# Attention over the memory with operands in rounded high and low parts

## What is computed

```
q = (h @ w_mq)      in 4 heads of 256
k = (mem_n @ w_mk), v = (mem_n @ w_mv)
p = softmax(q k^T * 256 ** -0.5)
y = (p v) @ w_mo
```

## Time and profile before

| | us |
|---|---|
| median of 3 runs | 900.39 |
| lowest, highest | 900.27, 903.83 |
| the profiled execution | 900.8 |
| its span, first to last instruction | 899.0 |
| PE busy in it | 883.5 (98%) |
| DVE busy, ACT busy | 574.6, 511.4 |

### The profile page before, as it was taken

The page is one execution under the profiler, slowest core; times in us unless marked ns, Lnnn a source line. Parts: engine busy times, 40 slices in busy tenths (PEclk is TensorE's granted clock), DMA queues, the critical chain, the costliest instruction groups (busy, mean ns, idle before and its releaser), DMA issues.

```text
span 899.0 us, 14674 instructions
## 1 busy us (share of the span) xinstructions
PE 883.5 (98%) x5696; PEld 783.3 (87%) x5696; DVE 574.6 (64%) x903; ACT 511.4 (57%) x937; POOL 90.2 (10%) x111
## 2 busy tenths in 40 slices
PE   8999999999999999999999999999999999999998
PEld 7898977898899998887778889988899789998886
DVE  6456666654676664445656999989846576664443
ACT  6466666665666553336558668797255466554330
POOL 0010000010000000001000413360152101000000
PEclk9999999999999999999999999999999999999999
DMA  9865324464456665555354644354430366655562
GB/s 331 301 198 203 141 96 141 140 212 94 151 178 193 195 222 199 198 188 187 130 199 149 197 145 149 115 185 141 114 134 1 120 206 186 193 188 187 189 198 80
DMA packets 110395, 152.22 MB, mean 169 GB/s; under 512 B 6752, under 2 KB 68344, under 8 KB 109944
## 3 DMA queue, kind: packets, MB, share of 16 engines
q1 hardware_dynamic: 110328, 151.31, 51.6%
HBM read 147.99 MB, written 3.30 MB: 168 GB/s over the span
## 4 chain that ended last, share of the span: by engine, by line
issue 47%; PE 33%; DVE 9%; ACT 3%; DMA 3%; POOL 2%; POOLq 1%; DVEq 1%; ACTq 0%; SPq 0%
PE acc L465 4%; PE acc L467 4%; PE acc L466 4%; PE acc L478 4%; PE acc L477 4%; PE acc L479 4%; DVE s_w_lo L415 3%; ACT s_w_hi L409 1%; DVE s_qkvT L1554 1%; PE acc L524 1%; PE acc L526 1%; PE acc L525 1%; DMA s_w_raw<-in_w_out 1%; POOLq L664 1%; ACT s_relu_i L1477 1%
## 5 line engine op out<-in xcount | busy, mean ns | idle before, releaser
L415 DVE TENSOR_TENSOR s_w_lo<-s_w_raw,s_w_hi 128x2048 fp32r<-128x2048 f32 (+1 forms) x201 | 313.1, 1574 | 170.1 <-ACT s_w_hi L409 169.8
L409 ACT ACTIVATE s_w_hi<-s_w_raw 128x2048 fp32r<-128x2048 f32 (+1 forms) x201 | 263.3, 1331 | 144.4 <-PE acc L467 100.7
L477 PE MATMUL acc<-s_h_hi,s_w_hi 128*128 128x256 f32 x784 | 218.6, 279 | 0.0
L478 PE MATMUL acc<-s_h_lo,s_w_hi 128*128 128x256 f32 x784 | 216.9, 277 | 0.0
L479 PE MATMUL acc<-s_h_hi,s_w_lo 128*128 128x256 f32 x784 | 216.9, 277 | 0.0
L477 PEld LDWEIGHTS acc<-s_h_hi,s_w_hi 128*128 128x128 f32 x784 | 147.4, 188 | 0.4
L478 PEld LDWEIGHTS acc<-s_h_lo,s_w_hi 128*128 128x128 f32 x784 | 147.3, 188 | 0.3
L479 PEld LDWEIGHTS acc<-s_h_hi,s_w_lo 128*128 128x128 f32 x784 | 147.2, 188 | 0.0
L466 PE MATMUL acc<-s_w_lo,s_hid_hi 128*128 128x512 f32 x224 | 87.1, 389 | 0.0
L467 PE MATMUL acc<-s_w_hi,s_hid_lo 128*128 128x512 f32 x224 | 87.1, 389 | 0.0
L465 PE MATMUL acc<-s_w_hi,s_hid_hi 128*128 128x512 f32 x224 | 87.1, 389 | 0.0
(11 more groups left out here) (334 smaller groups left out, 1459.1 us busy)
## 6 DMA issues: line engine op xcount, KB each, us to landing
s_w_raw<-in_w_in SPq DMA_DIRECT2D x43, 1024.0 KB, 5.2
s_w_raw<-in_w_ff SPq DMA_DIRECT2D x32, 1024.0 KB, 5.2
s_w_raw<-in_w_mlp_up SPq DMA_DIRECT2D x16, 1024.0 KB, 5.4
s_w_raw<-in_w_mlp_down SPq DMA_DIRECT2D x16, 1024.0 KB, 5.0
s_w_raw<-in_w_out SPq DMA_DIRECT2D x8, 1024.0 KB, 5.7
s_w_raw<-in_w_mk SPq DMA_DIRECT2D x4, 1024.0 KB, 5.7
s_w_raw<-in_w_mv SPq DMA_DIRECT2D x4, 1024.0 KB, 5.3
s_w_raw<-in_w_mq SPq DMA_DIRECT2D x4, 1024.0 KB, 5.2
```

Source lines behind the costliest of these rows:

```text
L409: act.activation(w_hi[u % SPLIT_SLOTS][:, cs], w_raw[u % RAW_SLOTS][:, cs], ACT.Copy).then_inc(w_hi_done, 4 if q is None else 1)
L415: dve.tensor_tensor(w_lo[u % RAW_SLOTS][:, cs], w_raw[u % RAW_SLOTS][:, cs], w_hi[u % SPLIT_SLOTS][:, cs].bitcast(F32), ALU.subtract).then ...
L477: pe.matmul(o, wh[:, cs], hi[:, k, :], start=k == 0, stop=False)
L478: pe.matmul(o, wh[:, cs], lo[:, k, :], start=False, stop=False)
```

## The change

Queries, keys, probabilities and values become high and low parts of type fp32r, and each product of the attention over the memory becomes three. The new buffers lie over others that are free by then (`mkT_hi` and `mkT_lo` over the normed memory `m_hi` and `m_lo`, `mv_hi` over keys and values of the first attention, `mv_lo` over its bias table).

- Keys: ACT rounds `mkT` in two instructions of 128x1024 ahead of `ff_act`, and DVE takes the remainder in two ahead of `ff_dve`.
- Values: ACT rounds `mv` in two of 128x1024 behind `ff_act`, ahead of the rounding of `mq[2]`. DVE's two remainders stand behind the one of `mq[2]`.
- Queries: ACT's copies out of PSUM now write `mqT_hi`. DVE gets four instructions for `mqT_lo`.
- Probabilities: DVE's copy (L850) becomes a copy on ACT (`PT_hi`) and a subtraction on DVE (`PT_lo`) behind it.
- PE: the first transposes of probabilities (pair 0) stand ahead of the scores of pair 1. Scores and values are 12 single-pass products for a pair in place of 4 of f32.

```diff
+        def mq_act_hi(act, j):
+            u = of["mq"][j]
+            act.wait_ge(unit_done, u + 1)
+            act.activation(mqT_hi[:, 2 * j:2 * j + 2, :], acc[units[u]["banks"][0]][:].rearrange("p (c s) -> p c s", c=2), ACT.Copy,
+                           scale=0.0625).then_inc(mq_hi, 1)
...
+        def mem_act_hi(act, keys, g):
+
+            if keys:
+                act.activation(mkT_hi[:, 4 * g:4 * g + 4, :], mkT[:, 4 * g:4 * g + 4, :], ACT.Copy).then_inc(mem_hi, 1)
+            else:
+                act.activation(mv_hi[:, g, :], mv[:, g, :], ACT.Copy).then_inc(mem_hi, 1)
...
+            for c in range(2):
+                k, ts = it["chunk"] + c, it["ts"]
+                pe.matmul(o, mqT_hi[:, k, ts], mkT_hi[:, k, :], start=c == 0, stop=False)
+                pe.matmul(o, mqT_lo[:, k, ts], mkT_hi[:, k, :], start=False, stop=False)
+                m = pe.matmul(o, mqT_hi[:, k, ts], mkT_lo[:, k, :], start=False, stop=c == 1)
...
+        def mem_act_copy(act, i):
+
+            act.wait_ge(pt_done, i + 2)
+            act.wait_ge(pv_done, i)
+            act.activation(PT_hi[:], PT_BANK.rearrange("p (j b s) -> p j b s", j=2, b=NT), ACT.Copy).then_inc(pt_hi, 2)
+
+        def mem_dve_copy(dve, i):
+
+            dve.wait_ge(pt_hi, i - I_MEM + 2)
+            dve.tensor_tensor(PT_lo[:], PT_BANK.rearrange("p (j b s) -> p j b s", j=2, b=NT), PT_hi[:].bitcast(F32),
+                              ALU.subtract).then_inc(ptc_done, 2)
...
+        def memory_act(act, between):
+            n = len(MEM) // 2
+            for p in range(n + 2):
+                if p == n - 1:
+                    mem_act_copy(act, I_MEM + 2 * p - 2)
+                    for j in (2 * p - 4, 2 * p - 3):
+                        at_act_out(act, I_MEM + j, MEM[j])
+                    for j in (2 * p, 2 * p + 1):
+                        at_act_exp(act, I_MEM + j, MEM[j])
...
             for g in range(2):
                 y_act(act, 1, g)
+            for g in range(2):
+                mem_act_hi(act, True, g)
             ff_act(act, "out", "p_out", "mpre")
+            for g in range(2):
+                mem_act_hi(act, False, g)
             advance_hi(act, of["mq"][0])
             mq_act_tile(act, 0)
...
+            dve.wait_ge(unit_done, of["mv"][-1] + 1)
+            for g in range(2):
+                mem_dve_lo(dve, True, g)
             ff_dve(dve, "out", "p_out", "mpre", 1)
-            for u in of["mq"][:-1]:
+            advance_lo(dve, of["mq"][0])
+            for g in range(2):
+                mem_dve_lo(dve, False, g)
+            for u in of["mq"][1:-1]:
                 advance_lo(dve, u)
+            mq_dve_tr(dve)
+            mq_dve_lo(dve, 2)
...
             mm("mq", 3, parts=[0])
             pe.wait_ge(mq_copied, NT)
+            pe.wait_ge(mem_lo, 4)
...
-            attention_pe(pe, MEM, I_MEM, between)
+            memory_pe(pe, between)
```

More of the change, by code:

```diff
@@ L266, in build_program @@
         r1.close()
+        e1 = ExitStack()
+        sb("under_parts", [P, 2 * S + 3 * S], at=e1)
+        PT_hi = sb("PT_hi", [P, 2, NT, P], F32R, at=e1)
+        mqT_hi = sb("mqT_hi", [P, KC, S], F32R, at=e1)
+        mqT_lo = sb("mqT_lo", [P, KC, S], F32R, at=e1)
+        mv_hi = sb("mv_hi", [P, NT, D], F32R, at=e1)
+        mv_lo = sb("mv_lo", [P, NT, D], F32R, at=e1)
+        sb("under_mkT", [P, NT * D], at=e1)
+        PT_lo = sb("PT_lo", [P, 2, NT, P], F32R, at=e1)
+        sb("under_m", [P, KC * S - 2 * NT * P + NT * D], at=e1)
+        mkT_hi = sb("mkT_hi", [P, KC, S], F32R, at=e1)
+        mkT_lo = sb("mkT_lo", [P, KC, S], F32R, at=e1)
+        e1.close()
         def hidden_buffers(tag, floats):
@@ new lines, in mem_pe_scores @@
+        def mem_pe_scores(pe, i, it):
+            pe.wait_ge(l_done, i - 1)
+            for u in it["units"]:
+                for b, n in released(u):
+                    pe.wait_ge(acc_free[b], n)
+            o = S_BANK[i % 2][:, 0:S]
+            for c in range(2):
[3 more added lines that the diff above has]
+                m = pe.matmul(o, mqT_hi[:, k, ts], mkT_lo[:, k, :], start=False, stop=c == 1)
+            m.then_inc(sc_done, 1)
@@ new lines, in mem_pe_pv @@
+        def mem_pe_pv(pe, i, its):
+            pe.wait_ge(ptc_done, i + 2)
+            pe.wait_ge(y_done, i)
+            for j, it in enumerate(its):
+                o = V_BANK[:, j * MD:(j + 1) * MD]
+                for b in range(NT):
+                    pe.matmul(o, PT_hi[:, j, b, :], mv_hi[:, b, it["vs"]], start=b == 0, stop=False)
+                    pe.matmul(o, PT_lo[:, j, b, :], mv_hi[:, b, it["vs"]], start=False, stop=False)
+                    m = pe.matmul(o, PT_hi[:, j, b, :], mv_lo[:, b, it["vs"]], start=False, stop=b == NT - 1)
+            m.then_inc(pv_done, 2)
@@ L1278, in build_program, with memory_dve @@
+        def memory_dve(dve, between):
+            n = len(MEM) // 2
+            for p in range(n + 1):
+                if p < n:
+                    for j in (2 * p, 2 * p + 1):
+                        at_dve_mask(dve, I_MEM + j, MEM[j])
+                if p >= 1:
+                    mem_dve_copy(dve, I_MEM + 2 * p - 2)
+                between(p)
         MEMU = [("mk", j) for j in range(4)] + [("mv", j) for j in range(4)]
```

60 lines of the change are left out of this document (52 added, 8 removed).

## The result

| | before | changed |
|---|---|---|
| median, us | 901.73 (4 runs) | 910.24 (4 runs) |
| all, us | 900.27, 900.39, 903.07, 903.83 | 907.24, 910.21, 910.26, 910.66 |
| profiled execution, its span | 900.8, 899.0 | 910.66, 908.9 |

The ratio is 1.0082, with a 95% interval from 1.0058 to 1.0106: slower, by under 1%. The medians are 8.5 us apart, about twice the 4.1 us of the prediction, and 910.24 lies outside its range.

What follows compares the result with a forecast made beforehand. It took PE, busy 883.5 of 899.0 us, to bound the kernel. The terms 1.98 + 1.5 + 0.44 - 0.35 + 0.5 = 4.1 us, added to the median of 900.39, gave 904.5 us, with an 8-in-10 range of 902.0 to 907.0.

Steps and rivals of the forecast that it cites:

- keys ahead of `out[2]`: Two key roundings on ACT ahead of `ff_act` delay PE's start of `out[2]` by 1.98 us.
- values ahead of `mq[2]`: Two value roundings on ACT ahead of the rounding of `mq[2]` make PE wait 1.5 us there.
- queries' remainders: At the first scores, DVE's subtractions behind ACT's two query copies make PE wait 0.44 us.
- first pair of scores: Twelve single-pass products in place of f32 save PE 0.35 us on the first pair's scores.
- attention from there on: From the last query product to the last values, PE comes out 0.5 us later.
- straight line between two row lengths: Price of a 128x1024 ACT rounding from rows of 512 and 2048: 1.06 us, taken as 0.99 each with overlap.
- two cases: At `mq[2]`, PE waits 1.74 us if DVE keeps its distance to ACT, 1.37 if that becomes 0.1.
- Rival 1: Roundings of keys and values are hidden and PE's savings of 2.8 us count: 897.6 us; chance 7%.
- Rival 2: In the attention, each of four pairs pays the ACT to DVE handover, 0.7 us in full: 906.8; chance 29%.
- Rival 3: ACT's 128x1024 instructions for keys and values don't overlap, 1.06 us each: 905.0 us; chance 12%.
- Rival 4: New products run in several passes, or PE's clock falls at a 2 us wait: well above 907; chance 1%.
- the last one of the sum: Behind the attention, PE hands the 4.1 us delay on to the end, being busy for 98% of the span.

Runs made afterwards that it cites:

- moved: Changed kernel with the keys' roundings between ACT's last two `h_hi` groups and the values' inside `ff_act`: 901.86 us, ratio 0.9996.
- low_last: moved, with products needing a low part last in their group and the queries' transposes in banks of their own: 901.13 us, ratio 0.9992.
- two_v_banks: low_last, with the values' products of every second pair in the bank `mq[3]` has left: 900.43 us, ratio 0.9985.
- changed_mid: Changed kernel plus one unread 16-column product behind the ninth unit of `ff1` and of `up`: 909.14 us, ratio 1.0072.
- v_banks_mid: two_v_banks plus one unread 16-column product behind the ninth unit of `ff1` and of `up`: 903.01 us, ratio 1.0014.
- before_mid: Kernel before plus one unread 16-column product behind the ninth unit of `ff1` and of `up`: 904.05 us, ratio 1.0025.
- breaks: Kernel before plus one unread 16-column product behind each of fourteen units of `ff1` and of `up`: 906.69 us, ratio 1.0040.
- swapped_order: Kernel before with the second and third of each chunk's three products exchanged in units with 256-wide products: 902.47 us, ratio 1.0002.

## Why the prediction was right and wrong

Start times on PE, before and changed, give each term of the sum. (The two stretches begin 0.08 us apart, which is taken off the first.)

| term | from the starts | predicted | measured |
|---|---|---|---|
| keys ahead of `out[2]` | 166.67, 168.64 | 1.98 | 1.89 |
| values ahead of `mq[2]` | 190.72, 193.92 | 1.5 | 1.23 |
| queries' remainders | 198.48, 202.13 | 0.44 | 0.45 |
| first pair of scores | 204.45, 207.91 | -0.35 | -0.19 |
| attention from there on | 226.86, 231.16 | 0.5 | 0.84 |
| sum | | 4.1 | 4.2 |

- *Keys.* Right, to the wait and its place. The Trainium skill ("ScalarE: Activation LUTs", section "Rules for kernel authors") would price each rounding at 1.15 us, an estimate by its rule. The trace has two in 2.02, so the rule is high by 0.14 for such neighbours, and the prediction's straight line between two row lengths was the better price.
- *Values.* Right in kind. The term was sized between two cases, and the lower one came true: DVE is 0.1 behind ACT, which is 1.37 by the prediction, and PE starts 0.15 behind DVE in place of 0.20.
- *Queries.* Right: DVE's two remainders run 200.78 to 202.07, and PE starts at 202.13.
- *First pair.* Mis-sized by 0.16: the twelve products take 1.53 us and not 1.37. 0.10 of that is the first step, 0.22 behind the wait, and 0.06 the other eleven at 0.119. The trace of before had offered both steps: 0.114 is a mean from 190.72 on the earlier trace rows, and the 34 steps from 200.32 to 204.33 are 0.118 each.
- *Attention.* The chain came out in the order that was worked out, and close to its instants (times from the last query product): maxima used at 3.4 (3.4), last scores 7.2 (7.2), second values 9.7 (9.6), third values 13.3 (13.1), `mo` 15.8 (15.5). The third values start behind `PT_lo`, 1.12 us of wait. Of the win of 0.35 at the last values 0.28 is left, by the step of 0.12. These two, 0.27 and 0.07, are what the term was short by.
- *Rival 1* (hidden) fell: nothing hid at the two places where the engines follow each other without a gap. moved shows that it can be had by another order.
- *Rival 2* (a handover in each pair) is right as a mechanism and didn't decide: the attention term is 0.84, just under its 0.9, and the pairs don't pay 0.7 each. low_last and two_v_banks took its remains away, 0.85 and 0.9 us of stretch in single profiles.
- *Rival 3* fell: two of 1024 take 2.02 us.
- *Rival 4*, its second half, was priced at 1% on "full clock in every slice" of a trace that has no wait of 2 us there. That row could not speak on a wait that the change itself makes. The fall is real: it adds 1.6 us in changed_mid, and the clock is low in 26 of the 60 executions with that wait. The 1% was far too low for it. It isn't the cause of the miss, since all four executions of the first comparison have full clock.

**The step that failed** is the last one of the sum: "Behind the attention the engines stand to each other as before, and PE hands the delay on to the end". The first half holds, since all of the further 5.6 us lie in `ff1` and `up`, where PE has no wait. The second doesn't: a PE that is never idle isn't a PE of one speed. `ff1` and `up` gave 5.6 us in the profiled executions, from 4.3 to 9.9 us of lateness, and that is the whole distance to the 910.66 of the profile (900.8 + 4.3 + 5.6). Beside it, the sum was added to a median of three executions, two of them in the fastest of before's three groups, as if that group were the kernel.

What the change itself costs, layers put even, is 4.0 us in the executions without a fall and 5.1 between medians (909.14 and 904.05). Over the four comparisons the ratios are 1.0082, 1.0041, 1.0065 and 1.0044, where 904.5 would have been 1.0046 of 900.39. That two of them lie next to it is in part luck, since ten of the 18 executions behind these two have a low clock. **Open** are three things: what decides in which step a layer begins (not the order of the products; an interruption changes it), whether the changed kernel begins in the long one more often than before (two of its four samples look so, with not one execution near 904.5 among twelve, and two don't), and why the clock falls behind the wait in some samples and never in others.

## What to carry to other kernels

Before work is put on an engine that prepares for the busiest one, look whether the chain there is already without a gap (a step of 0.41 where 0.23 is natural said so here), and put it instead into an idle time that the bracket of a row names: the same 2.02 us cost 1.9 us in one place and nothing in the other. Split products of 256 columns save 0.2 to 0.35 us for a pair here and need two more handovers, so order them such that the part that comes last is used last, and give the results a second bank. The whole of it gained 0.6 to 0.9 us of stretch, and 1.0 us between the medians of v_banks_mid and before_mid. Collect a dozen executions of both kernels before adding terms of a microsecond to a median, since untouched layers differed by 3 us each from one execution to the next, and look at the granted clock of each execution before a spread is put down to anything else.

## What the hardware showed that I had not expected

- Products 256 wide of fp32r run back to back in one of two lasting steps, 113.3 or 117.8 ns, at the same full clock and with no wait. In the long one every third weight load takes 192 ns, not 188. It lasted for all of the 623 steps of a layer's long run, and one product of 16 columns switched it, twelve times in a row in each of the two layers of breaks.
- The clock fell to its lower level about 1 us behind a wait of 1.91 us on PE and stayed there until about 173 (changed_mid). PE had been at full clock ahead of it, and had already taken up its products again when it fell. The granted clock is 0.998 or lower in 26 of 60 executions with such a wait, in none of 72 of the changed versions that avoid it, and in 5 of 143 of the kernel before.
- In swapped_order it fell behind a shorter wait, 1.07 us, and stayed low for longer, from about 661 to 675 us.
- Two roundings of 128x1024 from SBUF to SBUF on ACT take 2.02 us back to back, each time within 0.03.
